# First summands and fourth blocks loaded by GpSimd, and the fourth block ahead of the down chunk: one trunk of four layers on one core

## What is computed

```python
def swiglu(x, w_gate, w_up, w_down):
    return (jax.nn.silu(x @ w_gate) * (x @ w_up)) @ w_down

for i in range(DEPTH):
    x = x + 0.5 * swiglu(rms_norm(x, norm_g[i, 0]), ffn_w_gate[i, 0], ffn_w_up[i, 0], ffn_w_down[i, 0])
    h = rms_norm(x, norm_g[i, 1])
    q, k, v = jnp.split(h @ w_qkv[i], 3, axis=-1)
    ...
    x = x + mix @ w_o[i]
    x = x + 0.5 * swiglu(rms_norm(x, norm_g[i, 2]), ffn_w_gate[i, 1], ffn_w_up[i, 1], ffn_w_down[i, 1])
return rms_norm(x, final_g)
```

## Time and profile before

| | |
|---|---|
| median of 3 runs | 1882.12 us (1881.24 to 1883.84) |
| profiled run | 1877.97 us |
| span of its profile | 1876.2 us |
| TensorE products, busy | 1853.3 us (99%) |
| VectorE, busy | 1562.6 us (83%) |
| ScalarE, busy | 1166.9 us (62%) |
| GpSimd, busy | 60.3 us (3%) |
| granted TensorE clock | 0.999 of full |
| memory read | 414.74 MB, 222 GB/s over the span |

### The profile page before, as it was taken

One profiled execution on the slowest core, in us unless ns is written; L12 is line 12 of the kernel. 1 busy time (PEld: TensorE's weight loads), 2 busy tenths in 40 slices (PEclk: granted clock), 3 DMA queues, 4 the chain that ended last, 5 costly groups with the idle time before them and its releaser, 6 DMA issues.

```text
span 1876.2 us, 22732 instructions
## 1 busy us (share of the span) xinstructions
PE 1853.3 (99%) x9268; PEld 1566.1 (83%) x9268; DVE 1562.6 (83%) x1295; ACT 1166.9 (62%) x1220; POOL 60.3 (3%) x75
## 2 busy tenths in 40 slices
PE   9999999999999999999999999999999999999998
PEld 7788898888878899788888888987888888998886
DVE  7979568989888969998988995788898898569896
ACT  6666456666656645666665674465667567556665
POOL 1000000000000000100000000010000000001000
PEclk9999999999999999999999999999999999999999
DMA  8775445776677543577667763467775766437762
GB/s 300 261 290 226 180 157 180 226 289 264 200 249 272 235 151 134 183 254 286 266 187 272 255 247 121 149 227 245 270 278 190 274 221 246 157 108 252 277 238 79
DMA packets 59272, 417.28 MB, mean 222 GB/s; under 512 B 7192, under 2 KB 7456, under 8 KB 8992
## 3 DMA queue, kind: packets, MB, share of 16 engines
q1 hardware_dynamic: 53968, 380.09, 51.8%
q0 software_dynamic: 4608, 33.56, 9.5%
q10 hardware_dynamic: 592, 2.17, 0.3%
HBM read 414.74 MB, written 1.06 MB: 222 GB/s over the span
## 4 chain that ended last, share of the span: by engine, by line
PE 80%; DVE 12%; DMA 4%; ACT 2%; issue 2%; POOL 0%; SPq 0%; POOLq 0%; DVEq 0%; ACTq 0%
PE work L1493 16%; PE work L1495 16%; PE work L1494 16%; PE acc L1493 9%; PE acc L1495 9%; PE acc L1494 9%; DVE w_lo L919 6%; DMA extra<-stream_dram 3%; DMA raw<-stream_dram 1%; PE work L1687 1%; DVE raw L935 1%; PE acc L1537 1%; DVE raw L931 1%; PE work L1865 1%; PE work L1729 0%
## 5 line engine op out<-in xcount | busy, mean ns | idle before, releaser
L919 DVE TENSOR_TENSOR w_lo<-raw,w_hi 128x2048 fp32r<-128x2048 f32 x359 | 810.3, 2284 | 14.2 <-ACT w_hi L535 14.0
L535 ACT ACTIVATE w_hi<-raw 128x2048 fp32r<-128x2048 f32 x359 | 677.1, 1910 | 128.7 <-DVE raw L935 76.2
L1493 PE MATMUL work<-w_hi,xg 128*128 128x512 f32 x880 | 346.6, 394 | 1.1 <-DVE w_lo L919 1.1
L1495 PE MATMUL work<-w_hi,xg 128*128 128x512 f32 x880 | 343.5, 390 | 0.0
L1494 PE MATMUL work<-w_lo,xg 128*128 128x512 f32 x880 | 343.0, 390 | 0.0
L1493 PE MATMUL acc<-w_hi,m_hi 128*128 128x512 f32 x824 | 328.3, 398 | 6.3 <-DVE w_lo L919 6.1
L1495 PE MATMUL acc<-w_hi,m_lo 128*128 128x512 f32 x824 | 321.8, 391 | 0.0
L1494 PE MATMUL acc<-w_lo,m_hi 128*128 128x512 f32 x824 | 321.2, 390 | 0.0
L1495 PE MATMUL work<-w_hi,wide_r 128*128 128x512 f32 x512 | 199.8, 390 | 0.0
L1493 PEld LDWEIGHTS work<-w_hi,xg 128*128 128x128 f32 x880 | 165.4, 188 | 34.9 <-DVE w_lo L919 1.7
L1495 PEld LDWEIGHTS work<-w_hi,xg 128*128 128x128 f32 x880 | 165.3, 188 | 34.8
(11 more groups left out here) (211 smaller groups left out, 2324.8 us busy)
## 6 DMA issues: line engine op xcount, KB each, us to landing
raw<-stream_dram SPq DMA_DIRECT2D x295, 1024.0 KB, 7.3
extra<-stream_dram SPq DMA_DIRECT2D x64, 1024.0 KB, 4.9
extra<-stream_dram POOLq DMA_DIRECT2D x32, 1024.0 KB, 8.0
x<-x_dram SPq DMA_DIRECT2D x2, 512.0 KB, 8.2
raw<-stream_dram ACTq DMA_DIRECT2D x2, 512.0 KB, 8.0
scratch<-cum_rows ACTq DMA_DIRECT2D x1, 1024.0 KB, 6.5
cst<-consts_dram SPq DMA_DIRECT2D x1, 832.0 KB, 6.4
out_dram<-x SPq DMA_DIRECT2D x3, 256.0 KB, 2.5
```

Source lines behind the costliest of these rows:

```text
L535: nc.scalar.activation(w_hi[:, c % RING, :], raw_at(place), ACT.Copy).then_inc(hi_ready, 1)
L919: nc.vector.tensor_tensor(w_lo[:, c % RING, :], raw_at(place), w_hi[:, c % RING, :].bitcast(F32), ALU.subtract).then_inc(lo_ready, 1)
L1493: nc.tensor.matmul(dst, a_hi, b_hi, start=start, stop=False, skip_group_check=skip)
L1495: return nc.tensor.matmul(dst, a_lo, b_hi, start=False, stop=stop, skip_group_check=skip)
```

## The change

Fourth blocks and first summands leave SyncE's list, except the very first of each; GpSimd issues them, each first summand just ahead of its addition and the fourth block of the same pair behind. In the first pair of a chain b22 goes ahead of the down chunk and t4. Around these: in `first_of_chain` the gates take the order 11, 22, 12, 21, and the forms of the next pair's t3 and t2 come behind the last gate, which itself comes behind the splits of the next pair's t1 and b21; in unit 1, for all but the first feed-forward part, t3 is formed ahead of `hidden_lo(0)`; at the end of the differential attention one split is moved ahead of `apart_mean` on VectorE and ahead of `mix` on ScalarE, and the early updates behind the mean; the final norm reads `acc` in place of a scaled copy, with four times the epsilon.

```diff
 def pair_order(s):
@@
-    return [("b11", s), ("t1", s), ("t2", s), ("b21", s), ("t3", s), ("down", s - 1), ("t4", s), ("b22", s)]
+    return [("b11", s), ("t1", s), ("t2", s), ("b21", s), ("t3", s), ("b22", s), ("down", s - 1), ("t4", s)]
@@ plan
+            if what == "t4" and j in SEVEN[:-1] and not chained(following(j)):
+                loads.append(("b22", layer, n % 3, following(j), EXTRA, ("lo", c0 + order.index(("b22", j)) + 1)))
+            if what == "b21" and chained(j):
+                loads.append(("b22", layer, n % 3, j, EXTRA, ("lo", c0 + order.index(("b22", j - 2)) + 1)))
...
+SUMS_LOADS = [i for i, load in enumerate(LOADS) if load[4] == SUMS]
+EXTRA_LOADS = [i for i, load in enumerate(LOADS) if load[4] == EXTRA]
+SP_LOADS = [i for i, load in enumerate(LOADS) if load[4] < RAW or i in (SUMS_LOADS[0], EXTRA_LOADS[0])]
@@ sync
-            for i in range(RAW, EARLY_LOADS):
+            for i in SP_LOADS[RAW:EARLY_LOADS]:
...
-            for i in range(EARLY_LOADS, len(LOADS)):
+            for i in SP_LOADS[EARLY_LOADS:]:
@@ gpsimd
+            def free(i):
+                what, count = LOADS[i][5]
+                pool.wait_ge({"lo": lo_ready, "pv": pv_psum}[what], count)
+
+            def first_weight_sum(p):
+
+                if p:
+                    free(SUMS_LOADS[p])
+                    pool.dma_start(raw_at(SUMS), stream[SUMS_LOADS[p]]).then_inc(sums_loaded, 16)
+                    pool.wait_ge(sums_loaded, 16 * p)
+                else:
+                    pool.wait_ge(first_summand_loaded, 16)
+                pool.dma_start(raw_at(SUMS), stream[ADD_FROM[p]], accum_op=ALU.add).then_inc(t1_added, 16)
+
+            def fourth_block(p):
+
+                free(EXTRA_LOADS[p])
+                pool.dma_start(raw_at(EXTRA), stream[EXTRA_LOADS[p]]).then_inc(b22_loaded, 16)
@@
-                    first_weight_sums(n // 3 * 2 + n % 3 // 2)
+                    p = (n // 3 * 2 + n % 3 // 2) * len(SEVEN)
+                    if n == 0:
+                        first_weight_sum(0)
+                    for following_pair in range(p + 1, p + len(SEVEN) + (n % 3 == 2 and n < NORMS - 2)):
+                        first_weight_sum(following_pair)
+                        fourth_block(following_pair)
+                else:
+                    p = (n // 3 * 2 + 1) * len(SEVEN)
+                    first_weight_sum(p)
+                    fourth_block(p)
@@ vector, first_of_chain
-                        split_to(q + 5)
-                        if s == SEVEN[0]:
                             token_sums_lo((3,))
                         split_to(q + 6)
                         gate_11()
                         sum_22()
                         split_to(q + 7)
+                        sum_12()
                         split_to(q + 8)
                         gate_22()
-                        split_to(q + 9)
+                        gate_12()
+                        split_to(q + 10)
+                        gate_21()
                         form("t3", q + 8)
-                        gate_21()
-                        sum_12()
-                        split_to(q + 10)
                         form("t2", q + 8)
-                        gate_12()
                         hidden_lo(s)
                         split_to(q + 11)
@@ vector, end of the differential attention
                         apart_split(b)
+                        split_to(c0 + ATT_CHUNKS + 1)
+                        apart_mean()
                         for i in range(BANKS - 1):
                             early_update(i)
-                        apart_mean()
-                        split_to(c0 + ATT_CHUNKS + 1)
                         dve.wait_ge(r_apart_ready, 1)
@@ scalar, final norm
-                        update(n, i)
-                        square_sum(n, i)
+                        last_square_sum(i)
```

More of the change, by code:

```diff
@@ L85, in part_count, with block_count @@
     return [part for part, unit in pair_order(s) if unit == s].index(what) + 1
-def block_count(s, which):
-    return (("c11", "c22", "c12", "c21") if chained(s) else ("c11", "c22", "c21", "c12")).index(which) + 1
+def block_count(which):
+    return ("c11", "c22", "c12", "c21").index(which) + 1
 def sum_count(which):
@@ L451, in load @@
                 if free is not None:
-                    sp.wait_ge({"lo": lo_ready, "form": form_ready, "pv": pv_psum}[free[0]], free[1])
-                done = {EXTRA: b22_loaded, SUMS: sums_loaded}
+                    sp.wait_ge({"lo": lo_ready, "form": form_ready}[free[0]], free[1])
+                done = {EXTRA: first_b22_loaded, SUMS: first_summand_loaded}
                 sp.dma_start(raw_at(place), stream[i]).then_inc(done[place] if place in done else raw_loaded[place], 16)
@@ L460, in _ @@
                     sp.dma_start(gain[:], gains).then_inc(gain_loaded, 16)
-            for i in range(1, RAW):
+            for i in SP_LOADS[1:RAW]:
                 load(i)
             sp.dma_start(cst[:, 0:C_IDENT], consts[:, 0:C_IDENT]).then_inc(ones_loaded, 16)
-            for i in range(RAW, EARLY_LOADS):
+            for i in SP_LOADS[RAW:EARLY_LOADS]:
                 load(i)
@@ L531, in hi @@
                     act.wait_ge(form_ready, (no * len(SEVEN) + SEVEN.index(j)) * len(FORMS) + FORMS.index(what) + 1)
+                elif place < RAW:
+                    act.wait_ge(raw_loaded[place], 16 * count)
+                elif count == 1:
+                    act.wait_ge(first_b22_loaded, 16)
                 else:
-                    act.wait_ge(b22_loaded if place == EXTRA else raw_loaded[place], 16 * count)
+                    act.wait_ge(b22_loaded, 16 * (count - 1))
                 slot_free(act, c)
@@ L795, in attention @@
                         weights(b)
+                    if j == PAIRS and kind == DIFF:
+                        split_to(c0 + ATT_CHUNKS + 1)
                     if j < PAIRS:
@@ L1038, in plain_step @@
                     q = c0 + FFN_ORDER.index(("b11", s + 1))
-                    if s == 1:
+                    if s == 1 and n:
+                        token_sums_lo((0, 1, 2))
+                    elif s == 1:
                         token_sums_lo((0, 1))
@@ L1047, in plain_step @@
                     form("t3", q)
+                    if s == 1 and n:
+                        hidden_lo(0)
                     split_to(q)
@@ L1463, in final_mean @@
                 dve.wait_ge(squares_ready, BANKS * (NORMS - 1) + 2 * tb + 2)
-                nc.vector.scalar_tensor_tensor(out=mean[:, tb:tb + 1], in0=sums[:, 0, tb:tb + 1], scalar=EPS,
+                nc.vector.scalar_tensor_tensor(out=mean[:, tb:tb + 1], in0=sums[:, 0, tb:tb + 1], scalar=4 * EPS,
                                                in1=sums[:, 1, tb:tb + 1], op0=ALU.add,
@@ L1471, in final_output @@
                 dve.wait_ge(final_loaded, 16)
-                part = x_part(TB * half + tb)
-                nc.vector.scalar_tensor_tensor(out=part, in0=part, scalar=r_col[:, tb:tb + 1],
+                bank = TB * half + tb
+                nc.vector.scalar_tensor_tensor(out=x_part(bank), in0=acc[:, bank, :], scalar=r_col[:, tb:tb + 1],
                                                in1=final_gain[:, half * HALF_D:(half + 1) * HALF_D],
@@ L1670, in pair_step @@
                     quarter(chain, sum_of(S3), at["t3"], False, False)
+                    if s == SEVEN[0]:
+                        pe.wait_ge(token_lo_ready, BANKS * (f + 1))
+                    quarter(3, sum_of(S4), at["b22"], False, True)
                     unit_down(s - 1).then_inc(down_used, 1)
@@ L1673, in pair_step @@
                     quarter(chain, block_of(1, 1), at["t4"], False, True)
-                    if s == SEVEN[0]:
-                        pe.wait_ge(token_lo_ready, BANKS * (f + 1))
-                    quarter(3, sum_of(S4), at["b22"], False, True)
                 def pair_hidden(s):
@@ L1682, in pair_hidden @@
                     for block in ("c12", "c22") if second else ("c11", "c21"):
-                        pe.wait_ge(pair_h_ready, 4 * p + block_count(first, block))
+                        pe.wait_ge(pair_h_ready, 4 * p + block_count(block))
                     for t in range(2):
```

46 lines of the change are left out of this document (25 added, 21 removed).

## The result

The changed kernel takes **1865.71 us** by the median of 5 runs (1865.27 to 1866.78), the kernel before 1881.24 beside it (1874.98 to 1883.84, 5 runs). The ratio is 0.9919, with a 95% interval from 0.9903 to 0.9935: faster by 15.5 us.

The account below looks back on a forecast made before the run. TensorE, busy 1853.3 of 1876.2 us, was taken as the bound, so only its stalls could be won. Terms 10.7 + 1.5 + 0.5 = 12.7 us gave span 1863.5 and time 1869.4; range 1866.7 to 1877.5.

Parts of the forecast that it names:

- What bounds the kernel, and who is late: TensorE bounds the whole; in feed-forward passages VectorE's queue is late behind L931, which waits for the fourth block's load.
- The feed-forward term: TensorE's feed-forward waits for low weights and gated blocks go: 10.7 us, the middle between 9.1 (matmul side) and 12.5 (weight-load side).
- Differential attention: At its end, GpSimd's power runs without the split beside it, giving back 1.5 us of TensorE's 1.9 us wait for updated x.
- The end: Final norm: squares straight from acc drop a 0.60 us copy and the last power shortens: 0.5 us, at most 1.0.
- Unit 1: Form of t3 ahead of hidden_lo(0) fills 2.2 us of VectorE's 2.97 us idle, a further reserve for the pair; no gain summed.
- GpSimd costed at nothing: Loads moved to GpSimd: 54 us of issue off the path; possible norm delay costed at nothing, 0.5 us kept for the range.
- slower: Rival, chance 0.08: last gate waits behind t1's split and its two transfers, 2.1 us late in each of 16 passages: 1903 us.
- Half: Rival, chance 0.12: VectorE's backlog, not the load, is late; the down product still waits for w_lo: 1875.6 us.
- No change: Rival, chance 0.10: TensorE meets fourth block or down chunk before its low part; the 10.7 is lost, 2.0 remain: 1880.1 us.
- the last one, from the span to the time: Span forecast 1863.5 us became time 1869.4 by the difference between the profiled run's 1877.97 and the other three's median 1882.12.
- The low end: Lower end of the range: all weight-load waits and 1.0 at the end, 12.5 + 1.9 + 1.0 = 15.4 us, giving 1866.7.

Follow-up runs that it names:

- order alone: Kernel before with only the fourth block ahead of the down chunk and gates and sums ahead of the forms, SyncE issuing all loads: 1868.86 us, ratio 0.9939.
- GpSimd alone: Kernel before, old order of work, with first summands and fourth blocks issued by GpSimd: 1904.17 us, ratio 1.0129.
- SyncE held back: GpSimd issuing the loads on the old order, with SyncE waiting at the fourth block's old place until that block has landed: 1940.37 us, ratio 1.0322.
- doubled summand: Changed kernel with every first summand loaded twice by GpSimd, the second time after the first has landed: 1898.79 us.
- small edits: Kernel before with only the edits at the end of the differential attention and in the final norm: 1877.63 us, ratio 0.9985.
- doubled block: Changed kernel with every fourth block loaded twice by GpSimd, the second time after the first has landed: 1906.22 us.

## Why the prediction was right, and where it was wrong

**What bounds the kernel, and who is late: right.** The fourth block's landing on the old order and all that is queued behind L931 on VectorE; order alone gives 11.7 of the 15.5 us.

**The feed-forward term, 10.7: too large, by 0.5 to 1.7.** In the two profiled executions the span fell by 11.2; 1.7 of that is the wait for `x` and 0.5 the end, which leaves 9.0 for the feed-forward parts, just under the lower bound of 9.1 (matmul side), not in the middle. By the other four spans of after, 1863.8 in the middle, it is 10.2. The profiled execution of after is the heaviest of its five, and its trace shows where most of the missing 1.7 lies: the sum took all stops outside the start-up as gone, and 0.9 for `w_lo` and 0.3 for `pair_h` stay, with two new ones of 0.4 for `m_lo`. The order of events came as worked out: the block has 8.9 us in hand where 7 was claimed for that passage (3.0 at the tightest place, in unit 1, which the prediction didn't look at), the last gate is ahead of the form, and TensorE waits nowhere for b22, and for a down chunk only in that one place of 0.9.

**Differential attention, 1.5: right**, 1.7 by the wait, the power at 0.55. **The end, 0.5: right**, 7.5 to 7.0. Together 2.1 alone on the old order. **Unit 1, no price:** nothing of it shows in the sum, but the stop of 4.75 us above shows what that edit exposes.

**GpSimd costed at nothing: right as a sum, too easy as a reason.** The margin of the summand's chain was worked out as 21.8 less 16.9, 4.9 us; it is 4.2, but of other numbers, 18.2 less 14.0, as both ends and both landings differ from what was read. The doubled loads show that 5 to 8 us more on either chain cost 33 and 40 us. The stop near 100 us of the earlier trace rows went as forecast: 1.6 in the profile of before, 1.1 in order alone, gone with GpSimd. The threshold of the rival *slower* is not what its own terms give: 21.8 + 1.6 + 0.8 less 0.87, halved, is 11.7 us per transfer, and not 11.2. It changes no chance.

**The rivals.** *Half* did not come: VectorE's backlog alone would have kept the stops for `w_lo` ahead of down products, and they fell from 8.4 to 0.9. *No change* did not come either: new stops for the low part of the fourth block or of the down chunk are not in the trace of after. Beside it stood the Trainium skill's rule that DMAs spread over queues save only issue time, because all share the 16 engines (DMA: Bandwidth & Descriptors, "Rules for kernel authors"). No run here contradicts it: what the move gains on the new order, 1.5 us, is order, and what it costs on the old one, 23.6 us, is order too.

**The step that failed is the last one, from the span to the time.** The sum was 12.7, so 1876.2 became 1863.5; the span of after is 1863.4 to 1865.0. The prediction then wrote: "The profiled run took 1877.97, the median of the three others is 1882.12; the same difference gives 1869.4." It carried 4.15 us over unchanged. But that difference does not lie beside the stalls: it is more of them, in executions heavier than the profiled one, with the clock that one of them cost in the heaviest profile (3.0 + 1.6 us there), and the change removes that too. With only the constant 1.8 between span and time the same sum gives 1863.5 + 1.8 = 1865.3; measured 1865.71. What is left, 0.4, is of the size of the excess in the feed-forward term. The low end, built on the same 4.15 and the full 15.4, missed by 1.0. That three runs from 1881.24 to 1883.84 beside one of 1877.97 is much spread for a kernel on one core could be seen beforehand, and the prediction priced no variation of the waits.

Not settled: what makes the waits differ from one execution of before to the next. The median landings in the four profiles are alike (SyncE's chunk loads 7.0 to 7.1, GpSimd's additions 8.0 to 8.1), while VectorE's wait for the fourth block goes from 15.8 to 21.7.

## What to carry to other kernels

Where several runs differ by more than the change of a small term, ask first what the difference between them is made of: stall time that a change removes goes from every run, and the most from the slow ones, so the profile of one light run understates the gain. A load that is moved to another queue loses its place ahead of the loads that were issued behind it; find out what its wait held back, and move it only where the block has time in hand. Doubling one load is a cheap way to read a margin; the added load also slows its neighbours (an addition took 11.7 us in place of 8.6), so it can read lower than a count from the trace, and the price that it shows holds more than the one mechanism. A step that waits for a load delays all that is queued behind it, so look at what an earlier place for it puts at risk.

## What the runs showed of the hardware beyond that

A landing depends on what is on its way beside it more than on who issues it. GpSimd's first summand, with little beside it, took 5.1 us by the median; SyncE's 64 loads into the same two buffers took 4.9 in the kernel before. Its fourth block took 7.2 in the kernel with GpSimd alone, and 5.2 with SyncE held back. An addition took 8.6 where the block was issued 7.2 us behind it, and 11.7 where it was issued 1.7 behind.

TensorE's granted clock can fall behind a stop, and the length of the stop alone doesn't say whether it does. In one execution of the kernel before it was 0.69 over 5 us behind a stop of 2.40 us. Behind the stop of 4.75 us in the kernel with the doubled summand, the products behind it and the next stretch read:

```profile
800.00:806.00 6.00, 5.92 (x14) 4.69 (x15) 6.00 (x5) 3.79 (x3) 0.60 (x1) 0.50 0.03 5
806.00:812.00 6.00, 6.00 (x29) 4.95 (x29) 6.00 (x4) 2.34 (x3) 0.53 (x1) 0.99 0.61 197
```

0.50 is 1.2 GHz in place of 2.4: products start 0.43 us apart in place of 0.23, so that stop costs about 3 us (half of 6) beyond its own length. But the kernel with the small edits stops for 2.58 us ahead of 72.5 (counted as the 2.40 was), and its clock stays:

```profile
71.00:76.00 5.00, 3.51 (x17) 2.93 (x18) 5.00 (x5) 1.51 (x3) 0.88 (x1) 1.00 0.24 100
```

The same holds behind a stop of 2.99 us near 1306 us in the kernel with the doubled summand. And in the kernel with the doubled block the clock falls to 0.51 (1783.5 to 1787) at the end of a last stop of only 1.54 us, in a stretch in which TensorE had been busy for 3.44 of 5.5 us. So a stop can be dearer than its length; which ones are, these runs don't settle.
